# The second attention's output projection starts with another pair of tiles, on the other half of the tokens

## The reference

```python
def first_block(x, c, ...):
    for layer in range(DEPTH):
        shift, scale, gate = ...            # from c @ mod_w
        h = rms_norm(x, norm_w[layer, 0, 0]) * (1.0 + scale) + shift
        y = mixer_cd(h, w_in_cd[i], w_out_cd[i], rel_table)     # layer 1
        x = x + gate * rms_norm(y, norm_w[layer, 0, 1])
        ...                                  # then the feed-forward part
```

## Time and profile before

| what | value |
|---|---|
| median of 3 runs | 1258.65 us (1257.03 to 1263.89) |
| profiled execution | 1258.39 us, its span 1256.6 us |
| mean granted TensorE clock | 0.967 |
| PE busy | 1159.3 us, 92% of the span |
| DVE busy | 933.0 us, 74% |
| ACT busy | 589.3 us, 47% |
| chain that ended last | PE 72%, DVE 17%, DMA 5%, ACT 5% |

### The profile page before, as it was taken

The page is one execution under the profiler, slowest core; times in us unless marked ns, Lnnn a source line. Parts: engine busy times, 40 slices in busy tenths (PEclk is TensorE's granted clock), DMA queues, the critical chain, the costliest instruction groups (busy, mean ns, idle before and its releaser), DMA issues.

```text
span 1256.6 us, 19977 instructions
## 1 busy us (share of the span) xinstructions
PE 1159.3 (92%) x8358; PEld 1049.2 (83%) x8358; DVE 933.0 (74%) x1630; ACT 589.3 (47%) x968; POOL 74.7 (6%) x106
## 2 busy tenths in 40 slices
PE   2788888999998997899999989999989989999996
PEld 1677568999897995799999979999979967999996
DVE  5967868888786966689888688886765957765445
ACT  1534665444345457553445464444443365444433
POOL 0000000000000000088000000000000000000000
PEclk8799899999999998999999999999999998999998
DMA  9991434888883870467789547779732452765730
GB/s 374 359 369 52 171 135 176 298 316 315 277 334 144 325 262 20 148 235 272 302 229 361 213 165 298 302 248 316 277 118 102 108 178 87 261 243 197 189 131 34
DMA packets 40810, 280.83 MB, mean 223 GB/s; under 512 B 4736, under 2 KB 5264, under 8 KB 7952
## 3 DMA queue, kind: packets, MB, share of 16 engines
q1 hardware_dynamic: 37296, 269.27, 59.4%
q0 software_dynamic: 2416, 7.92, 2.0%
q10 hardware_dynamic: 1008, 2.37, 0.6%
HBM read 277.91 MB, written 1.10 MB: 222 GB/s over the span
## 4 chain that ended last, share of the span: by engine, by line
PE 72%; DVE 17%; DMA 5%; ACT 5%; issue 1%; SPq 0%; DVEq 0%; ACTq 0%
PE PS L408 71%; DVE LO L1382 5%; DMA raw<-WS 4%; DVE raw L1372 3%; ACT HI L954 2%; DMA SC<-scratch 1%; DVE TMP L1482 1%; DVE SC L1586 1%; DVE TMP L1447 1%; DVE HLo L1442 1%; ACT SQ L954 1%; DVE SC L1571 1%; ACT HH L954 1%; ACT SC L954 0%; DVE RS L1586 0%
## 5 line engine op out<-in xcount | busy, mean ns | idle before, releaser
L408 PE MATMUL PS<-HH,HI 128*128 128x256 f32 x1748 | 501.6, 287 | 26.0 <-ACT HH L954 22.3
L408 PE MATMUL PS<-HLo,HI 128*128 128x256 f32 x1748 | 502.8, 288 | 0.5 <-DVE HLo L1442 0.2
L408 PE MATMUL PS<-HH,LO 128*128 128x256 f32 x1748 | 498.8, 285 | 0.0
L1382 DVE TENSOR_TENSOR LO<-raw,HI 128x1024 fp32r<-128x1024 f32 x340 | 403.9, 1225 | 113.4 <-ACT HI L954 113.3
L954 ACT ACTIVATE HI<-raw 128x1024 fp32r<-128x1024 f32 x340 | 339.9, 1048 | 95.4 <-PE PS L408 63.1
L408 PEld LDWEIGHTS PS<-HH,HI 128*128 128x128 f32 x1748 | 339.5, 194 | 35.2 <-DVE LO L1382 19.3
L408 PEld LDWEIGHTS PS<-HH,LO 128*128 128x128 f32 x1748 | 339.5, 194 | 3.4 <-issue 0.5
L408 PEld LDWEIGHTS PS<-HLo,HI 128*128 128x128 f32 x1748 | 338.9, 194 | 4.0 <-DVE HLo L1442 2.8
L1372 DVE CUSTOM_DVE_ANT_0 raw<-raw,CB,SM 128x1024 f32<-128x1024 f32 x168 | 210.5, 1284 | 24.5 <-DMA raw<-WS 24.3
L408 PE MATMUL PS<-HI,HDH 128*128 128x512 f32 x352 | 140.2, 398 | 0.0
L408 PE MATMUL PS<-HI,HDL 128*128 128x512 f32 x352 | 139.5, 396 | 0.0
(11 more groups left out here) (235 smaller groups left out, 1022.9 us busy)
## 6 DMA issues: line engine op xcount, KB each, us to landing
raw<-WS SPq DMA_DIRECT2D x255, 1024.0 KB, 5.5
SC<-scratch POOLq DMA_DIRECT2D x2, 1024.0 KB, 13.8
FB<-gates_out POOLq DMA_DIRECT2D x3, 512.0 KB, 4.9
SQ<-gates_out POOLq DMA_DIRECT2D x3, 512.0 KB, 9.6
X<-xT ACTq DMA_DIRECT2D x1, 1024.0 KB, 6.8
SC<-ssm POOLq DMA_DIRECT2D x2, 512.0 KB, 4.3
out<-TMP SPq DMA_DIRECT2D x2, 512.0 KB, 2.6
CB<-vecs SPq DMA_DIRECT2D x1, 512.0 KB, 6.4
```

Of the source, the lines that this page charges most:

```text
L408: return e.matmul(o, l, r, start=start, stop=stop, skip_group_check=True)
L1382: e.tensor_tensor(LO[:, s % HL, :], raw_half(j, h), HI[:, s % HL, :].bitcast(fp32), O.subtract).then_inc(*D.up(("lo", s)))
```

## The change

The chunks of the output matrix are streamed in the order 2, 0, 1, 3, so that the weights of tiles 4 and 5 come first. PE runs tiles 4 and 5 on qt 1, then tiles 4 and 5 on qt 0, then tiles 0, 1, 2, 3, 6, 7 on qt 0, then the same six on qt 1. `out_half` gets two more arguments: `gives`, the qt on which a half unit is given back, and `begins`, the tile that opens the accumulation. The first call waits only for HLo of tile 7, which in DVE's order stands ahead of that of tiles 0 to 3; the second waits for HLo of tile 3 as well. ACT and DVE split the half units in the new order of tiles, as far ahead as before. The other two output projections keep their order. The number of instructions on each engine is the same.

```diff
-    plan += weave(ws("cd", 9), mods(20, 4), 0) + ws("cdo", 4)
+    plan += weave(ws("cd", 9), mods(20, 4), 0) + [("w", ("cdo", i)) for i in (2, 0, 1, 3)]
...
-            def out_half(name, ks, qt):
+            def out_half(name, ks, qt, gives=1, begins=0):
 
                 for k in ks:
                     key = (name, k // 2)
                     wt = weight(key, k % 2)
                     w.wait_ge(*A.at(("hh", name, k)))
-                    w.wait_ge(*D.at(("hlo", name, 7 if qt else max(k, 3))))
-                    rows(name, (HH, HLo), k, wt, k == 0, k == 7, [used(key, k % 2)] if qt else [], (qt,))
+                    w.wait_ge(*D.at(("hlo", name, 7 if qt or begins else max(k, 3))))
+                    if begins and not qt:
+                        w.wait_ge(*D.at(("hlo", name, 3)))
+                    rows(name, (HH, HLo), k, wt, k == begins, k == 7, [used(key, k % 2)] if qt == gives else [],
+                         (qt,))
...
-            out_half("cdo", (0, 1, 2, 3, 4, 5), 0)
-            out_half("cdo", (0, 1), 1)
-            out_half("cdo", (6, 7), 0)
-            out_half("cdo", range(2, 8), 1)
+            out_half("cdo", (4, 5), 1, 0, 4)
+            out_half("cdo", (4, 5), 0, 0, 4)
+            out_half("cdo", (0, 1, 2, 3, 6, 7), 0, 1, 4)
+            out_half("cdo", (0, 1, 2, 3, 6, 7), 1, 1, 4)
...
             def linear_out(name, ks, beyond=0):
-                for k in ks:
-                    use((name, k // 2), k % 2, min(AHEAD, 7 - k + beyond))
+                for i, k in enumerate(ks):
+                    use((name, k // 2), k % 2, min(AHEAD, 7 - (i if len(ks) == 8 else k) + beyond))
...
-            linear_out("cdo", range(8))
+            linear_out("cdo", (4, 5, 0, 1, 2, 3, 6, 7))
```

## The result

| | before | changed |
|---|---|---|
| median of 20 runs each | 1259.63 us (1257.03 to 1264.69) | 1255.39 us (1253.37 to 1257.23) |
| ratio, with 95% interval | | 0.9962 (0.9953 to 0.9971) |
| span of the profiled execution | 1256.6 us | 1253.3 us |
| mean granted clock | 0.967 | 0.966 |

The ratio is 4.8 us of 1259.63. The kernel is a little faster, clear of the noise and within the 0.5% that was called "no change to speak of" ahead of the run. The prediction was 1253.8 us and 4.9 us of gain.

A forecast was written before the change was run, and what follows sets the result against it. PE was taken as the bound, with 72% of the path that sets the end. Closing two holes and keeping the clock up (2.1 + 1.3 + 1.4 = 4.8, taken as 4.9) gave 1258.65 - 4.9 = 1253.8 us; range 1250.5 to 1258.5.

The forecast's parts named there:

- The first hole: PE idle 2.11 us between the last MoBA values and the second attention's projection, awaiting HLo copies; goes entirely.
- The second hole: PE idle ahead of the projection's 49th matmul, awaiting tile 6's split weights; 1.11 us, 1.27 by starts; goes.
- No new wait: Split weights of tiles 2 and 3 are ready before PE wants them in the projection, margins 1.2 and 1.3 us.
- The clock: PE's lower clock in the projection's first seven matmuls loses 1.43 us; expected to stay at 1.00 after the change.
- the three terms: The first hole, the second hole and the clock in the projection: 2.1 + 1.3 + 1.4 = 4.8 us.
- The sum: From the end of the MoBA values to the projection's end, 26.8 us become 21.9: gain 4.9 us.
- the third term: The clock in the projection, 1.43 us, read from the one profiled run.
- case 3: PE's low clock at the entry of f1 gets better too: 1252.2 to 1250.8 us, chance 0.18.
- case 2: Both holes go, but a low clock stretch still falls on the projection or a later entry: 1255.4 us, chance 0.27.

The follow-up runs named there:

- the late copies: Changed kernel with two idle ACT passes ahead of its copies of tiles 0 to 3; 33.16 us from the last MoBA values to f1's first product.
- the first trial: Changed kernel, but tiles 4 and 5 run on qt 0 only after tiles 0 to 3; ratio to the kernel before 1.0001.
- filling the hole: Kernel before with 16 matmuls of zeros between the MoBA values and the projection; ratios to the kernel before 1.0002 and 0.9999.
- second hole only: Kernel before, but tiles 0 and 1 run on qt 1 directly behind their qt 0; ratio to the kernel before 0.9993.
- late start: Changed kernel, but tiles 4 and 5 on qt 1 wait for all four copies; ratio to the kernel before 0.9995.

## Why the prediction was right

**The first hole.** Predicted: 2.1 us, entirely. Right. The profile shows no idle time there, and putting the wait back costs 2.12 us of distance. The copies of tiles 0 to 3 end at 496.13 and the 13th matmul starts at 496.99, 0.86 us behind, for a predicted 0.8; the late copies give 0.8 too.

**The second hole.** Predicted: 1.27 us. Right within about 0.1 us: putting it back into the changed kernel costs 1.39 us (34.00 - 32.61), and closing it alone gave 1.20 beside a fall of the clock that was 0.2 us dearer.

**No new wait.** Right in the changed kernel, and the first trial shows how near it is: the same chain, tile 2 wanted 12 matmuls earlier, gives 1.52 us of waiting. All margins held because ACT's HI does start where the prediction read it, directly behind its second table load.

**The clock.** Predicted: 1.43 us, with bounds from 0 to 1.7 lost again. In the profiles it is just that: filling the hole takes 1.38 us off the distance, and the three terms, each changed by itself, add up to the whole (2.12 + 1.39 + 1.38 = 4.89, for 4.90 measured). As a term of the median it isn't shown. For it: the changed kernel's gain is 4.7 ± 0.36 us, the two holes are worth 3.5 of it (2.12 + 1.39), and the clock is the nearest thing to give the other 1.2, since the matmuls are the same in number and kind; that is argued, not shown. Against it: filling the hole, which holds the clock there in both profiles, gains 0.0 ± 0.45, and the first trial, with the clock at 1.00 in its profile, gains 0.5 ± 0.7, which is what its waits alone give (0.6) rather than its profile (1.7). The rest may lie in the clock at other places. Which of the two isn't settled.

The Trainium skill (TensorE: Matmul & The Clock Gate, "What's actually happening") has the monitoring run freely of the kernel. The profiles are in keeping with this, without showing it for one kernel: the same hole behind the same work met the lower level in one and not in another (second hole only, late start), at 1.58 us.

**The sum.** 4.9 predicted, 4.8 measured by the ratio. The two holes are the part of it that was understood; that the total met the third term as well, which was read from one execution, is in part luck. The time itself came out 1.6 us over the 1253.8, in the range; 1.0 of it is the median of before, which rose from 1258.65 with 3 runs to 1259.63 with 20. In the profiled execution what case 3 names did happen in part (a shorter low stretch at f1), and so did what case 2 names (a new one at f2), and they nearly cancelled. But neither is tied to the change: kernels that begin the projection as late as before show the same pair.

**The step that failed** isn't in the prediction but behind it: the expectation for the first trial moved a tile forward without asking when its weight would be ready.

## What to carry to other kernels

Where a projection must wait for the copies of its input, look for a part of the input that is ready and whose accumulator is free: here one half of the tokens accumulates in the very banks whose content is copied first. Order a resident set so that what is given back early is what the next load waits for; two tiles on both halves at once return their slots after 18 matmuls in place of 42. And for each such move write down when every later operand is wanted and when it is ready: closing a wait shortens all distances behind it.

## What was not expected of the hardware

The same 2.11 us hole behind 1.08 us of work leaves the clock at 1.00 in one profile (late start) and drops it to 0.51 in another (second hole only), worth 1.58 us in a projection of 22. And a filling that shows 1.38 us in two profiles shows 0.0 ± 0.45 us in the total of 24 runs. The low stretches at two later entries come as a pair, long at f1 and none at f2 or shorter at f1 and one at f2, in kernels with and without the change. With a clock that may fall at several places, a local gain of clock read in one profile can't be added to a sum of waits without more runs.
